# Expert rows of two tiles gathered during the other tiles' phases, and one dense expert sweep of four tiles instead of two of three

## The reference

```python
xn = rms_norm(h, norm_mix_g)                     # 1: mixers
z = xn @ w_in                                    # 1024 x 4352
oa = diff_attn(dq, dk, dv, lam)                  # 4 heads, two softmax maps each, chunk-causal
ob = window_attn(sq, sk, sv, sinks)              # 8 q heads, 2 kv heads, window 128
h = h + (ga * (oa @ w_a) + gb * (ob @ w_b)) @ w_out
h = h + mem_attn(rms_norm(h, norm_mem_g), mk, mv, w_q, w_o)      # 2: 256 memory tokens
...
def peer(xn):                                    # 3: experts
    q = (xn @ w_q).reshape(n, 8, 2, 64)
    v1, i1 = top_k(q[:, :, 0] @ keys1, 16); v2, i2 = top_k(q[:, :, 1] @ keys2, 16)
    sc, sel = top_k(all sums v1 + v2, 16); idx = the 16 expert numbers i1 * 128 + i2
    g = softmax(sc)
    hid = einsum('nd,nhkd->nhk', xn, u[idx])     # u, v: 16384 x 1024
    return einsum('nhk,nhkd->nd', gelu(hid) * g, v[idx])
```

## Time and profile before

| what | us |
|---|---|
| median of 3 runs | 4570.38 |
| the runs | 4570.34, 4570.38, 4610.2 |
| the profiled execution, its own time | 4569.48 |
| its span in the trace | 4567.7 |
| PE busy in the span | 4049.8 (89%) |
| DVE busy | 2861.7 (63%) |
| ACT busy | 1447.8 (32%) |
| POOL busy | 979.8 (21%) |
| moved by DMA | 905.89 MB, mean 198 GB/s |

### The profile page before, as it was taken

One profiled execution on the slowest core, in us unless ns is written; L12 is line 12 of the kernel. 1 busy time (PEld: TensorE's weight loads), 2 busy tenths in 40 slices (PEclk: granted clock), 3 DMA queues, 4 the chain that ended last, 5 costly groups with the idle time before them and its releaser, 6 DMA issues. The chain is left out here.

```text
span 4567.7 us, 60721 instructions
## 1 busy us (share of the span) xinstructions
PE 4049.8 (89%) x19923; PEld 3409.7 (75%) x19923; DVE 2861.7 (63%) x5530; ACT 1447.8 (32%) x2567; POOL 979.8 (21%) x811
## 2 busy tenths in 40 slices
PE   6999798978878756878559999999999999999996
PEld 5788566734456655777548999999999999999996
DVE  4300354311122098888858888888888888888886
ACT  3111233311112113544443333333333333333333
POOL 0000000000000000000004444444444444444441
PEclk9999899789989777888779999999999999999998
DMA  4322421120040100122129999999999999999995
GB/s 142 116 87 79 117 70 42 41 110 28 19 166 0 42 3 11 78 106 124 78 116 378 341 340 340 339 340 339 340 339 340 339 340 339 339 339 341 336 340 212
DMA packets 387884, 905.89 MB, mean 198 GB/s; under 512 B 41664, under 2 KB 185024, under 8 KB 386496
## 3 DMA queue, kind: packets, MB, share of 16 engines
q1 hardware_dynamic: 257696, 491.80, 30.1%
q0 software_dynamic: 110656, 403.62, 25.1%
q10 hardware_dynamic: 19440, 9.44, 0.7%
HBM read 815.62 MB, written 90.18 MB: 198 GB/s over the span
## 5 line engine op out<-in xcount | busy, mean ns | idle before, releaser
L1968 POOL DMA_INDIRECT exp_gu<-in_peer_u_rows,exp_gidx x384 | 487.0, 1268 | 1372.7 <-DMA exp_ggate<-s_ggate 828.9
L2099 PE MATMUL exp_h<-exp_xh,exp_uh 128*128 128x384 f32 x2048 | 688.1, 336 | 47.5 <-DVE exp_ul L2020 47.5
L2101 PE MATMUL exp_h<-exp_xh,exp_ul 128*128 128x384 f32 x2048 | 688.4, 336 | 0.0
L2100 PE MATMUL exp_h<-exp_xl,exp_uh 128*128 128x384 f32 x2048 | 687.1, 335 | 0.0
L2112 PE MATMUL exp_y<-exp_vh,exp_al 128*128 128x512 f32 x1536 | 602.7, 392 | 0.0
L1974 POOL DMA_INDIRECT exp_gv<-in_peer_v,exp_gidx x384 | 473.0, 1232 | 602.4 <-DVE H L2035 520.0
L2111 PE MATMUL exp_y<-exp_vl,exp_ah 128*128 128x512 f32 x1536 | 602.1, 392 | 0.0
L2110 PE MATMUL exp_y<-exp_vh,exp_ah 128*128 128x512 f32 x1536 | 597.2, 389 | 0.0
L1987 ACT ACTIVATE exp_gel<-exp_h 128x384 f32<-128x384 f32 x256 | 126.0, 492 | 1372.7 <-PE exp_h L2101 1372.7
L2035 DVE SCALAR_TENSOR_TENSOR H<-exp_gv,exp_coef,H 128x1024 f32<-128x1024 f32 x384 | 470.6, 1281 | 10.0 <-issue 0.4
L2025 DVE CUSTOM_DVE_ANT_0 exp_gu<-exp_gu,exp_xg 128x1024 f32<-128x1024 f32 x384 | 449.6, 1222 | 0.0
(11 more groups left out here) (293 smaller groups left out, 5982.8 us busy)
## 6 DMA issues: line engine op xcount, KB each, us to landing
exp_u<-in_peer_u SPq DMA_DIRECT2D x256, 512.0 KB, 5.9
exp_v<-in_peer_v SPq DMA_DIRECT2D x256, 512.0 KB, 6.2
exp_w<-s_w SPq DMA_DIRECT2D x256, 192.0 KB, 6.4
out_z<-proj_zs SPq DMA_DIRECT2D x72, 256.0 KB, 2.0
proj_w<-in_w_in SPq DMA_DIRECT2D x16, 1024.0 KB, 5.4
merge_gates<-out_z SPq DMA_DIRECT2D x9, 1024.0 KB, 5.1
s_zt<-proj_zt ACTq DMA_DIRECT2D x27, 256.0 KB, 2.3
exp_gu<-in_peer_u_rows,exp_gidx POOLq DMA_INDIRECT x384, 6.3
```

The costliest lines, as they stand in the source:

```text
L1968: pool.indirect_dma_start(out=gu[i % 2][t][:, :], out_offset=None, in_=I["peer_u_rows"], in_offset=bass.IndirectOffsetOnAxis(ap=gidx[:, t, ...
L2099: pe.matmul(hp[s][:, 0:TC], uh[s][:, c, :], xh[k][:, c, :], start=(c == 0), stop=False)
L2100: pe.matmul(hp[s][:, 0:TC], uh[s][:, c, :], xl[k][:, c, :], start=False, stop=False)
L2101: last = pe.matmul(hp[s][:, 0:TC], ul[s][:, c, :], xh[k][:, c, :], start=False, stop=(c == KD - 1))
```

## The change

Tiles 0 and 1 ("early" tiles, NE = 2) go through project, diff, window, merge, memory and the choosing part of retrieve alone. Their lists, gates and normalized rows stay on the core. Then the other seven ("late") tiles go through all these phases. While they do, POOL gathers the u rows of the two early tiles (2 x 128 gathers of 512 KB) and DVE makes their dots: 140 in project, 84 in diff and 32 in window (DOTS). ACT makes the gelu, and then the v rows are gathered and DVE makes 256 axpys: 24 in window, 124 in merge and 108 in memory (AXPYS). Places for gathered rows ("ring") are the H rows of the seven late tiles, which hold nothing needed until merge reloads x into them; in merge seven and in memory five rows of their own. Several instruction loops of these phases are written out, the buffers of w_in are split in two, and the semaphores are released at eight places instead of three, each with two barriers of all engines.

In the expert phase three tiles (2 to 4) are listed and gathered as before, and four (5 to 8) are dense. One sweep of 128 steps takes all four: TC = 512 columns in each hidden product and weight block. Every step has three dots and three axpys. Six PSUM banks add up the output of three dense tiles as before; the hidden values have one bank, where they had two, and the eighth bank (exp_spare) takes the fourth tile's output in two halves a step, each of which DVE adds to H (add_half) before the bank is written again. In spread the matrix operand top_right is laid out with the 128 elements of one product side by side.

```diff
-PHASES = [
-    ({}, [phase_project]),
-    ({"OA": [P, NT, CW], "OB": [P, NT, CW], "sso": [P, NH * NT]}, [phase_diff, phase_window, phase_merge]),
-    ({}, [phase_memory, phase_retrieve, phase_experts, phase_final]),
-]
+DOTS = (140, 84, 32)
+AXPYS = (24, 124, 108)
+MERGE_SLOTS, MEMORY_SLOTS = 7, 3
...
+            phase_project(nc, sem, K, I, S, *early)
...
+            phase_retrieve(nc, sem, K, I, S, *early, NE)
+            release()
+            K["ring"] = [K["H"][:, t, :] for t in range(NE, NT)]
+            phase_project(nc, sem, K, I, S, *late, dots[0])
...
+                phase_diff(nc, sem, K, I, S, *late, dots[1])
+                phase_window(nc, sem, K, I, S, *late, dots[2], axpys[0])
+                phase_merge(nc, sem, K, I, S, *late, axpys[1], MERGE_SLOTS)
+            release()
+            phase_memory(nc, sem, K, I, S, *late, axpys[2], MEMORY_SLOTS)
+            release()
+        phase_retrieve(nc, sem, K, I, S, *late, NG)
+        release()
+        phase_experts(nc, sem, K, I, S)
...
+def fetch(pool, K, table, ring, came, used, units):
+    for j, u in enumerate(units):
+        if j >= len(ring):
+            pool.wait_ge(used, j - len(ring) + 1)
+        pool.indirect_dma_start(out=ring[j % len(ring)], out_offset=None, in_=table,
...
+def dot(dve, K, ring, came, used, units, j):
+    u, row = units[j], ring[j % len(ring)]
+    dve.wait_ge(came[j % len(ring)], 16 * (j // len(ring) + 1))
+    dve.tensor_tensor_reduce(out=row, in0=row, in1=K["xg"][:, u % NE, :], scale=1.0, scalar=0.0, op0=ALU.mult, op1=ALU.add,
...
-        right = [sb(f"right{r}", [P, NKEY, OH]) for r in range(2)]
+            right = [sb(f"right{r}", [P, OH, NKEY]) for r in range(2)]
...
+                def add_half(q, half):
+                    dve.wait_ge(half_ready, q * 2 + half + 1)
+                    dst = H[:, NT - 1, half * CW:(half + 1) * CW]
+                    dve.tensor_tensor(dst, dst, spare[:, :], ALU.add).then_inc(half_added, 1)
...
+                    if not first:
+                        add_half(q - 1, 1)
                     if further:
                         low_u(q + 2, s)
...
+                    dot(s, turn, 0)
+                    dot(s, turn, 1)
+                    add_half(q, 0)
+                    dot(s, turn, 2)
+                    if not first:
+                        axpy(q - 1, 1 - s, turn_before)
...
-                def hidden(q, s, k, first=False):
+                def hidden(q, s, first=False):
                     pe.wait_ge(ul_ready, q + 1)
                     if not first:
-                        pe.wait_ge(h_taken, q - 1)
+                        pe.wait_ge(h_taken, q)
...
+                    if not opens:
+                        pe.wait_ge(half_added, q * 2)
+                    product(spare, s, ND - 1, 0, True, True).then_inc(half_ready, 1)
                     for x in range(NY):
...
+                        product(yp[x], s, x // 2, x % 2, opens, closes)
+                    pe.wait_ge(half_added, q * 2 + 1)
+                    product(spare, s, ND - 1, 1, True, True).then_inc(half_ready, 1)
```

More of the change, by code:

```diff
@@ L454, in phase_diff, with width_of, group @@
         o_done = sem("diff_o_done")
-        OA = K["OA"]
-        groups = [1, 1, 1, 1, 2, 2, 2, 2, 1]
-        NG = sum(groups)
+        OA, ring = K["OA"], K["ring"]
+        came, used = [sem(f"diff_came{r}") for r in range(len(ring))], sem("diff_used")
+        tiles = range(base, base + n)
+        groups = [1 if t < 4 or t == NT - 1 else 2 for t in tiles]
+        NGR = sum(groups)
+        total = NH * n
+        loads = 16 * (7 if samples_too else 4)
+        made = 10 if samples_too else 7
+        def width_of(t):
+            return (t + 1) * P if t < NT - 1 else NKS
+        def group(g, c):
+            return g // n * NGR + sum(groups[:g % n]) + c
         def diag(ap):
@@ L683, with phase_window @@
+                for x in range(total + 2):
+                    if x % n == 0 and x < total:
+                        pe.wait_ge(loaded[x // n % 2], (x // n // 2 + 1) * loads)
+                    if x < total:
+                        scores(x)
+                    if 1 <= x <= total:
+                        turn(x - 1)
+                    if x >= 2:
+                        values(x - 2)
 NPAIR = 4
 NKW = P + TS
-def phase_window(nc, sem, K, I, S):
+def phase_window(nc, sem, K, I, S, base, n, dots=(), axpys=()):
@@ L728, in phase_window, with width_of @@
         new_rows = sem("win_new_rows")
-        OB = K["OB"]
+        OB, ring = K["OB"], K["ring"]
+        came, used = [sem(f"win_came{r}") for r in range(len(ring))], sem("win_used")
+        row_in, row_used = [sem(f"win_row_in{r}") for r in range(len(ring))], sem("win_row_used")
+        acts_ready = sem("win_acts_ready")
+        total = NPAIR * n
+        loads = 16 * (7 if samples_too else 4)
+        made = 11 if samples_too else 9
+        turning = total * len(dots) // max(1, len(dots) + len(axpys))
+        def width_of(t):
+            return P if t == 0 else 2 * P if t < NT - 1 else NKW
         def diag(ap):
@@ new lines, in _ @@
+                for x in range(total + 2):
+                    if samples_too and x % n == 0 and x < total:
+                        samples(x // n)
+                    if x < total:
+                        maxima(x)
+                    if x >= 2:
+                        finish(x - 2)
+                    while j < min(len(dots), len(dots) * (x + 1) // max(1, turning)):
+                        dot(dve, K, ring, came, used, dots, j)
+                        j += 1
+                    if axpys and x == turning + 2:
+                        dve.wait_ge(acts_ready, 1)
+                        dve.tensor_tensor(K["dots"][:, :, :], K["dots"][:, :, :], K["ggate"][:, :, :], ALU.mult)
+                        dve.drain()
+                    while x >= turning + 2 and m < len(axpys) * (x - turning - 1) // (total - turning):
+                        axpy(dve, K, ring, row_in, row_used, axpys, m)
+                        m += 1
@@ L965, in phase_merge @@
         junk = sb("junk", [P, D])
+        ring = [sb(f"row{r}", [P, D])[:, :] for r in range(slots)]
         tp = [ps(f"t{a}", [P, 4, P]) for a in range(2)]
@@ L1065, in merged @@
                     dve.drain()
[L1066 removed]
+                    if t > 0:
                         dve.wait_ge(t_ready, 4 * t + 2)
@@ L1173, in phase_memory @@
         junk = sb("junk", [P, D])
+        ring = [sb(f"row{r}", [P, D])[:, :] for r in range(slots)]
+        if slots:
+            ring += [K["xg"][:, t, :] for t in range(NE)]
         tp = ps("t", [P, KD, P])
@@ L1263, in _ @@
                 exponents(0)
-                with act.Fori(1, NT - 1) as t:
+                for t in range(1, n):
                     copy_probs(t - 1)
@@ L2076, in _ @@
                 low_u(1, 1)
[L2077 to L2088 removed]
+                step(0, 0, 0, 0, first=True)
```

1733 lines of the change are left out of this document (904 added, 829 removed).

## The result

| what | before | changed |
|---|---|---|
| median, us | 4585.94 (4 runs, 4570.34 to 4610.2) | 4242.55 (4 runs, 4241.24 to 4243.71) |
| ratio, 95% interval | | 0.9239 [0.9197, 0.9281] |
| span of the profiled execution, us | 4567.7 | 4240.4 |
| DVE busy in it | 2861.7 (63%) | 3193.4 (75%) |
| PE busy in it | 4049.8 (89%) | 3276.6 (77%) |

The change is faster by 7.6%, 343 us by the medians and 327 by the two spans: the runs of before spread over 40 us, and the profiled one lies at their lower end. Forecast were 4116 us and a gain of 453: the time is 126 us late, inside the range (4040 to 4255), near its upper end.

A forecast was written before the change was run, and what follows sets the result against it. PE was taken to bound the sweep, DVE after the change. Project +18, diff +68, window +46, merge +24, memory +37, retrieve -120, experts -538, releases +12 make -453 from 4569.5: 4116 us, range 4040 to 4255.

The forecast's parts named there:

- The sweep: Expert phase: 128 steps of 12.4 us, DVE slowest with a sum of 12.29, 1616 us against 2154: -538.
- rival (c): Sweep: PE's clock falls as PE waits twice a step; 48 products take 22.0 us, total 5345 us; chance 0.04.
- the stretch of memory in the earlier trace: Memory, 1345 to 1470 us: PE 13% idle at clock 1.00, cited against a lost clock in the sweep.
- Rival (a): Sweep: DMA bounds it at 337 GB/s, step 13.2 us, total 4218 us; chance 0.18.
- The early rows: Early tiles' dots and axpys in late phases: project 0, diff 50, window 32, merge 9, memory 20 us.
- rival (b): Early tiles' rows not hidden: diff and window cost 162 instead of 82, merge and memory some 40 more, 4236 us; chance 0.23.
- I let half be hidden behind PE's waits: Diff: of 96 us of early tiles' dots, 50 us taken as added time, bounds 0 and 96.
- close to being the chain itself: Diff: DVE idles some 0.5 us between prompt tiles, where two or three dots of 2.3 to 3.4 us stand.
- Starting twice: Project, diff, window, merge, memory pay their start again: 18, 18, 14, 15 and 17 us, sum 82, between 0 and 203.
- Retrieve: Two dense tiles less and dense batches of 3.1 instead of 3.73 us: 699 against 819 us, -120.
- DVE and ACT now read their source with strides, which costs something: Retrieve: reason for taking a batch at 3.1 us, with DVE next at 2.8; no row shows the cost.
- Rival (d): Retrieve: the new operand layout gives nothing, since 0.233 us a product has another reason; +40, 4156 us; chance 0.09.

The follow-up runs named there:

- small_add: Changed kernel with each half addition in the sweep on 16 of 512 columns: 4109.41 us, one run; step 11.25 instead of 12.28 us.
- old_right: Changed kernel with only the layout of top_right undone, its 128 elements of one product apart as before: 4254.76 us.

## Why the prediction was right, and what missed

**The sweep** was right in its mechanism and its size: PE gives the bound to DVE, 12.28 us a step against a sum of 12.29, and the phase gained 549 us against 538. From start to start PE's 48 products leave 1.3 us a step, as forecast (the view's 27 us without work in 400, 0.8 a step, are fewer, since busy times count the overlapping end of a product), and its clock stayed at 1.00; rival (c) did not come, as the stretch of memory in the earlier trace rows had said. Rival (a) is refuted by small_add.

**The early rows** were the mis-sized term, as in rival (b): I took 50, 32, 9 and 20 us for diff, window, merge and memory and none for project, 111 in all; the runs show 91, 28, 17, 54 and 6, together 196. The step that failed in diff was "I let half be hidden behind PE's waits": the order had shown that the dots stand where DVE hardly waits; of their 96 us, 61 come back when their DVE time alone is taken away, and 91 when the gathers go too, with PE's clock at 0.93 instead of 0.81. Nor was DVE "close to being the chain itself" there: before, PE was busy for 204 of diff's 235 us and DVE for 122; it is the dots that put DVE on the chain. In memory, the excess of axpys over the two waits was counted (2.6 us a tile), but not the 40.6 us in which DVE waits for gathers in a ring of five rows; the prediction had named this wait as a sign of being wrong. The sum had no term for the gathers' effect on other transfers, nor for the lower clock of the late phases.

**Starting twice** was taken at 82 us and 12 for the releases; without the rows, four of the five phases show 109, and project 18 less the 6 us of its rows, 121 in all. Window is the largest miss, 38 against 14: its early pass runs at clock 0.50 from end to end, and its late pass without the rows takes 161 us for seven tiles at 0.67, where nine took 171 at 0.76; the row with 0.76 could have warned of it.

**Retrieve**: 34 us short, and 64 batches x (3.63 - 3.1) = 34. PE's part came out as forecast; "DVE and ACT now read their source with strides, which costs something" was the term, and it took nearly all of the gain. Rival (d) named the loss but not its reason: PE's product did become cheap, and DVE took its place.

**The range** held the time because its upper end came from rivals (a) and (b). The forecast's own sum missed by 126 us, and all its larger misses point the same way, so the hit is owed in part to the width of the range.

## What to carry to other kernels

Work that is moved beside a chain of short steps is hidden only where its engine waits, so look in the order for the place of each piece, and fill the long waits, not the short ones. When an operand's layout is turned for one engine, the stride moves into the work of the engine that makes it: price both. A phase's first gathers run beside its own first loads and delay them.

## What the runs showed of the hardware

- An addition on POOL with two inputs in SBUF held up the DVE instruction that met it: 2.31 us instead of 1.21 for a dot, 1.42 instead of 0.69 for a product. The Trainium skill, "SBUF — State Buffer", section "SBUF: two separate sides", tells of a port pair that the two engines lock in turn for a whole instruction; the rows agree.
- A drain of POOL behind an addition, with gathers under way, let the next gather start 5.46 us late; without it, 0.15 us.
- A multiplication on DVE of 768 bf16 elements a partition that reads with a stride took 1.52 us in the changed kernel, 0.95 with neighbouring elements in old_right; the layout that it writes and the order in which its second operand repeats changed with it.
- 397 GB/s were sustained over 400 us by one core, in small_add's sweep.
